# Row sums turned through DRAM and spread by a transfer, in a float32 transformer pair on one core

## The reference, cut to what matters

```python
sh1, sc1, g1, sh2, sc2, g2 = split(silu(c) @ w_mod + b_mod)      # 2048 values each
h = rms_norm(x, norm_g[0]) * (1 + sc1) + sh1
x = x + g1 * rms_norm(fourier_mix(h) @ fnet_w_out, norm_g[1])
h = rms_norm(x, norm_g[2]) * (1 + sc2) + sh2
x = x + g2 * rms_norm(square(relu(h @ w_mlp_in)) @ w_mlp_out, norm_g[3])
# second block, FoX heads: causal, so queries 0..127 see keys 0..127 only
logits = q @ k.T * scale + c[q] - c[k];  p = softmax(where(causal, logits, -inf));  o = p @ v
```

## Time and profile before

| | us |
|---|---|
| median of 3 runs | 2137.29 (2136.57 to 2138.25) |
| the profiled execution | 2136.71 |
| its span in the trace | 2135.0 |
| PE busy in it | 2092.3 |
| DVE busy | 1356.6 |
| ACT busy | 994.9 |
| TensorE clock granted, mean | 0.997 |

### The profile page before, as it was taken

One profiled execution on the slowest core, in us unless ns is written; L12 is line 12 of the kernel. 1 busy time (PEld: TensorE's weight loads), 2 busy tenths in 40 slices (PEclk: granted clock), 3 DMA queues, 4 the chain that ended last, 5 costly groups with the idle time before them and its releaser, 6 DMA issues.

```text
span 2135.0 us, 29831 instructions
## 1 busy us (share of the span) xinstructions
PE 2092.3 (98%) x11099; PEld 1762.9 (83%) x11099; DVE 1356.6 (64%) x1350; ACT 994.9 (47%) x1282; POOL 59.2 (3%) x95
## 2 busy tenths in 40 slices
PE   5999999999999999999999999999999999999999
PEld 3767878888888888887988888888888888888887
DVE  3878988887655655656767476555645655554563
ACT  4344364444543444444554567554434434343442
POOL 0010000110000000001100000000000000000000
PEclk9999999999999999999999999999999999999999
DMA  9999988887667667666665555566566656656654
GB/s 387 379 393 397 371 320 329 305 303 259 223 213 213 214 213 221 207 223 199 207 179 158 149 159 186 190 185 187 191 193 188 191 192 189 191 191 194 189 189 156
DMA packets 222842, 492.26 MB, mean 231 GB/s; under 512 B 15148, under 2 KB 15528, under 8 KB 221976
## 3 DMA queue, kind: packets, MB, share of 16 engines
q1 hardware_dynamic: 211956, 450.98, 64.9%
q0 software_dynamic: 10112, 38.79, 5.4%
q10 hardware_dynamic: 676, 1.14, 0.1%
HBM read 485.61 MB, written 5.25 MB: 230 GB/s over the span
## 4 chain that ended last, share of the span: by engine, by line
PE 87%; DVE 5%; DMA 2%; ACT 2%; issue 2%; SPq 1%; DVEq 0%; ACTq 0%
PE ps L559 43%; PE ps L521 22%; PE ps L526 11%; DVE acc L1662 3%; DMA raw<-in_w_mod_dram 2%; PE ps L543 1%; PE ps L544 1%; PE ps L545 1%; PE ps L608 1%; DMA raw<-in_w_mem_kv_dram 1%; PE ps L821 1%; PE ps L820 1%; PE ps L819 1%; PE ps L967 1%; SPq L310 1%
## 5 line engine op out<-in xcount | busy, mean ns | idle before, releaser
L1637 DVE TENSOR_TENSOR wl<-raw,wh 128x1024 fp32r<-128x1024 f32 x684 | 810.4, 1222 | 283.6 <-ACT wh L1140 281.5
L1140 ACT ACTIVATE wh<-raw 128x1024 fp32r<-128x1024 f32 x684 | 697.4, 1054 | 526.2 <-DMA raw<-in_w_down_dram 159.9
L521 PE MATMUL ps<-xt,wh 128*128 128x512 f32 x2048 | 643.7, 396 | 1.4 <-DVE xt L1897 1.4
L559 PE MATMUL ps<-wh,u 128*128 128x512 f32 x2176 | 585.1, 389 | 1.0 <-DVE u L2224 0.6
L559 PEld LDWEIGHTS ps<-wh,u 128*128 128x128 f32 x2176 | 407.3, 188 | 85.8 <-DVE u L2224 1.0
L526 PEld LDWEIGHTS ps<-xt,wl 128*128 128x128 f32 x2048 | 384.7, 188 | 90.9
L526 PE MATMUL ps<-xt,wl 128*128 128x256 f32 x2048 | 402.3, 278 | 0.0
L559 PE MATMUL ps<-wl,u 128*128 128x512 f32 x1088 | 335.2, 389 | 0.0
L521 PEld LDWEIGHTS ps<-xt,wh 128*128 128x128 f32 x2048 | 312.2, 189 | 2.8 <-issue 2.4
L559 PE MATMUL ps<-wh,xt 128*128 128x512 f32 x960 | 269.0, 394 | 3.9 <-DVE wl L1637 2.6
L559 PEld LDWEIGHTS ps<-wl,u 128*128 128x128 f32 x1088 | 204.2, 188 | 42.5
(11 more groups left out here) (303 smaller groups left out, 1493.0 us busy)
## 6 DMA issues: line engine op xcount, KB each, us to landing
raw<-in_w_mlp_in_dram SPq DMA_DIRECT2D x128, 512.0 KB, 4.0
raw<-in_w_mlp_out_dram SPq DMA_DIRECT2D x128, 512.0 KB, 4.3
raw<-in_w_up_dram SPq DMA_DIRECT2D x128, 512.0 KB, 3.8
raw<-in_w_down_dram SPq DMA_DIRECT2D x128, 512.0 KB, 3.6
raw<-in_w_mod_dram SPq DMA_DIRECT2D x126, 512.0 KB, 10.5
raw<-in_w_in_dram SPq DMA_DIRECT2D x96, 512.0 KB, 3.8
slot<-in_w_mod_dram POOLq DMA_DIRECT2D x32, 512.0 KB, 5.2
raw<-in_w_out_dram SPq DMA_DIRECT2D x32, 512.0 KB, 3.6
```

What stands on the lines that cost most here:

```text
L521: mm(ps[:, 4 * par + j, :], wh[:, at, t, j * P:(j + 1) * P], flat(xt[:, kt, :, :]), start=kt == 0, stop=kt == KT - 1, skip_group_check=True)
L559: last = mm(o, act[:, kt, z, half * P:(half + 1) * P], w, start=kt == 0 and n == 0, stop=kt == KT - 1 and n == 2, skip_group_check=True)
L1140: A(flat(wh[:, i, :, :]), tile_at(landed[0]), ACT.Copy).then_inc(sem("w_hi"), 1)
L1637: V.tensor_tensor(flat(low_at(s)), tile_at(s), flat(wh[:, i, :, :]).bitcast(F32), ALU.subtract).then_inc(sem("w_lo"), 1)
```

## The change

Sums of partial rows are made as rows: `row_sum` multiplies the accumulator by a 128 x 32 block of ones, two products of 512 columns side by side in two column quadrants. ACT copies the rows to SBUF (`summed_row`), POOL writes them to DRAM and reads them back one value per partition (`turned_row`: `shift_row` for `s2`, `bias_row` for `hb`). The gates are summed by four products side by side in one bank; DVE copies four rows (`gate_row`), POOL writes them to DRAM and reads them back into all 128 partitions (`gate_spread`), and DVE multiplies in SBUF. PE's second `mod_rows` of sh2 is gone (DVE sums those four tiles), all four first groups run without the shift (so 32 tiles are summed again, by a table), the side tiles of g2 start four groups later, sh2's first tiles are loaded ahead of the first chunks, ACT squares before it rounds the first two chunks, and the FoX heads leave out keys 128..255 for queries 0..127.

```diff
-SH2_QUADS = tuple(n for n in range(32) if n // QUAD in (0, 4))
-AGAIN = [(0, kt) for kt in range(KT)] + [(1, kt) for kt in range(KT // 2, KT)]
+SH2_QUADS = tuple(n for n in range(32) if n // QUAD == 0)
+AGAIN = [(pair, kt) for pair in range(2) for kt in range(KT)]
+AGAIN_AT = [{1: 0, 3: 1, 5: 2, 7: 3}, {1: 4, 3: 5, 5: 6, 7: 7}, {1: 8, 3: 9, 5: 10, 7: 11}, {1: 12, 3: 13, 5: 14, 7: 15},
+            {1: 16, 2: 17, 3: 18, 5: 19, 6: 20, 7: 21}, {1: 22, 2: 23, 3: 24, 5: 25, 6: 26, 7: 27}, {0: 28, 1: 29, 2: 30, 3: 31}]
-        TAIL = ([("chunk", j) for j in range(4)] + [("tile", n) for n in range(4)]
+        TAIL = ([("tile", n) for n in range(4)] + [("chunk", j) for j in range(4)]
...
+            def gate_spread(k):
+                pool.wait_ge(sem("gate_row"), k + 1)
+                pool.dma_start(gate_dram[k].rearrange("(j n) -> j n", n=GC), acc[0][0:P:QP, 0:GC]).then_inc(sem("gate_kept"), 16)
+                pool.wait_ge(sem("gate_kept"), 16 * (k + 1))
+                pool.dma_start(acc[0][:, :], gate_dram[k:k + 1, :].to_broadcast([P, D])).then_inc(sem("gate_in"), 16)
...
+            def turned_row(k, dst, src, scratch, half):
+                pool.wait_ge(sem("turn_rows"), k + 1)
+                if k:
+                    pool.wait_ge(sem("turn_in"), 16 * k)
+                pool.dma_start(scratch[half].rearrange("(j n) -> j n", n=GC),
+                               src[0:2 * QP:QP, half * MODC:half * MODC + GC]).then_inc(sem("turn_out"), 16)
+                pool.wait_ge(sem("turn_out"), 16 * (k + 1))
+                pool.dma_start(dst[:, half * CH:(half + 1) * CH], scratch[half].rearrange("(c p) -> p c", p=P),
+                               allow_slow_non_contiguous=True).then_inc(sem("turn_in"), 16)
...
-                for n, b in enumerate(banks):
-                    last = mm(ps[:, b, :], ones[:, :], acc[a][:, n * GC:(n + 1) * GC], start=True, stop=True)
+                for j in range(QUAD):
+                    last = mm(ps[j * QP:(j + 1) * QP, bank, :], ones[:, 0:QP], acc[0][:, j * GC:(j + 1) * GC], start=True, stop=True,
+                              skip_group_check=True, tile_position=(0, j * QP))
...
+            def row_sum(t, half, bank):
+                for j in range(2):
+                    last = mm(ps[j * QP:(j + 1) * QP, bank, :], ones[:, 0:QP], t[:, half * MODC + j * GC:half * MODC + (j + 1) * GC],
+                              start=True, stop=True, skip_group_check=True, tile_position=(0, j * QP))
+                last.then_inc(sem("turn_mm"), 1)
...
             def shifted_hi(r):
-                act.wait_ge(sem("a2_ready"), 2 + r // 2)
-                act.wait_ge(sem("chunk_used"), CH * G_ML1 + (12, 12, 30, 32)[r])
+                act.wait_ge(sem("turn_in"), 16 * (r // 2 + 1))
+                act.wait_ge(sem("chunk_used"), CH * G_ML1 + (28, 28, 30, 32)[r])
...
+            def summed_row(k, t, half, bank):
+                act.wait_ge(sem("turn_mm"), k + 1)
+                A(t[0:2 * QP, half * MODC:half * MODC + GC], ps[0:2 * QP, bank, :], ACT.Copy).then_inc(sem("turn_rows"), 1)
...
-                act.wait_ge(sem("hb_ready"), g // 2 + 1)
+                act.wait_ge(sem("turn_in"), 16 * (g // 2 + 3))
...
+            def gate_row(k, bank):
+                dve.wait_ge(sem("gate_mm"), k + 1)
+                V.tensor_copy(acc[0][:, 0:GC], ps[:, bank, :]).then_inc(sem("gate_row"), 1)
...
-                    if (g, i) in ((0, 6), (1, 1)):
-                        gate(0, (4, 6), 0, (g,))
+                    if (g, i) == (0, 6):
+                        gate_row(0, 4)
+                    if (g, i) in ((1, 2), (1, 5)):
+                        gate(0, 0, i // 5)
...
                         if j == 2:
-                            gate(1, (2, 6), 2 + MODN, (0,))
+                            gate_row(1, 2)
                         lo(4 + j, 4 + j, m0 + (j + 1))
+                    gate(1, 2 + MODN, 0)
                     return
...
+            def keys_of(name, tb):
+                return (tb + 1) * P if name == "fox" else S
```

More of the change, by code:

```diff
@@ L775, in first_beside @@
                     transposes(1, h, (2 + i,), drained="x1t_out")
-                if (g, i) == (1, 4):
+                if (g, i) == (1, 5):
                     pe.wait_ge(*mod_used(mod_c(C_SH2, KT - 1)))
                     pe.wait_ge(sem("evacuated"), G_ML1 + 1)
[L779 to L782, removed]
+                    row_sum(acc2, 0, 0)
                 if (g, i) == (3, 5):
@@ L785, in first_beside @@
                     pe.wait_ge(sem("evacuated"), G_ML1 + 3)
-                    mod_sum(2, 0, (1,))
-            def again_sum(pair):
[L790 to L794, removed]
+                    row_sum(acc2, 1, 0)
+            def row_sum(t, half, bank):
[3 more added lines that the diff above has]
+                last.then_inc(sem("turn_mm"), 1)
+            def again_sum(pair):
+                pe.wait_ge(sem("again_used"), KT * (pair + 1))
+                row_sum(acc[1], pair, 2 + pair)
             def mlp(G0, build, ups, between=None):
@@ L1027, in att_pv @@
                     for hd in range(4):
[L1028 removed]
+                        n = keys_of(name, tb) // P
+                        for sb_ in range(n):
                             last = mm(ps[:, 4 + tb, hd * P:(hd + 1) * P], pt[:, hd, sb_, tb * P:(tb + 1) * P], val(sb_, hd),
[L1030 removed]
+                                      start=sb_ == 0 and hd == 0, stop=sb_ == n - 1, skip_group_check=True)
                 last.then_inc(sem(name + "_pv"), 1)
@@ L1148, in hi_run @@
                 for j in range(CH):
-                    if between and j < 5:
+                    if between:
                         between(j)
@@ L1539, in soft_exp @@
                 for j in range(8):
-                    A(pr[:, j, :], pr[:, j, :], ACT.Exp, bias=nmx[:, j:j + 1],
+                    n = P if name == "fox" and j % 2 == 0 else S
+                    A(pr[:, j, 0:n], pr[:, j, 0:n], ACT.Exp, bias=nmx[:, j:j + 1],
                       accum_out=sm[:, j:j + 1]).then_inc(sem(name + "_e"), 1)
@@ L1939, in mlp_up, with mlp_down @@
                                 ALU.subtract).then_inc(sem("u_lo"), 1)
-            def mlp_down(G0, s, p, e, side, onto, first=False, last=False, tail=False, between=None):
+            def mlp_down(G0, s, p, e, side, onto, first=False, last=False, tail=False, between=None, sides=()):
                 m0 = s * 32 + p * 16 + (CH * (G0 + e) + 4)
@@ L2084, in mlp1_first @@
                         held_lo(3)
-                with dve.Fori(0, 2) as p:
-                    for e in range(2):
-                        mlp_down(G_ML1, 3, p, e, True, y)
+                for g in range(GQ):
+                    n = 2 * GQ + 2 * g
+                    mlp_down(G_ML1, 3, g // 2, g % 2, True, y, between=lambda j: side_tile(n) if j == 3 else None, sides=(n + 1,))
             def out_lo(g):
```

164 lines of the change are left out of this document (92 added, 72 removed).

## The result

The changed kernel takes 2145.44 us (median of 6 runs, 2142.77 to 2148.70) against 2137.05 for the kernel before (6 runs, 2136.55 to 2138.57): ratio 1.0035, 95% interval 1.0025 to 1.0045. That is slower by 8.4 us or 0.39% by the medians (0.35% by the ratio), where the forecast had +10.0 us; the total lies 1.3 us under the forecast of 2146.7. The total was right; two of its six terms were far off, and they cancelled.

What follows compares the result with a forecast made beforehand. PE, busy 98% of the span, was taken as the bound; +1.8 - 4.6 + 7.1 + 1.4 + 6.5 - 2.2 = +10.0 us on 2136.7 gave 2146.7, own range 2141.8 to 2152, with two in ten outside 2131 to 2155.

Steps and rivals of the forecast that it cites:

- PE work removed: First MLP loses sh2's second `mod_rows` (1.85) and 0.68 in each of four sums, -4.6 us; FoX heads -2.2 us.
- First gate and seam: Before the first MLP: DVE waits 4.8 us for the gate's trip, x1's turns start at 279.8 instead of 278.0, +1.8 us.
- The shift: Second half's 10.3 us trip stalls PE 5.3 us at chunk (4, 4), plus 1.8 half clock: +7.1 us, bounds 0 and 11.
- Tiles summed again: Groups with six tiles through two buffers: 6.9 us a cycle, 55 us against 57, PE wait of 1.4 us.
- rival (c): Load queue becomes the bound in groups with six tiles, cycle 8.3 us, 9 late: +8 us, 2155; chance 0.10.
- Second gate: Tail of the first MLP: an 11 us trip holds DVE, PE stalls 7 us, +6.5 us; bounds -2.1 and +9.
- (b): Rival: only the gates wait, the shift and the tiles summed again are covered: +1.5 us, 2138.2; chance 0.15.
- DVE's wait at the first gate: Profile sign: DVE idle 4 to 6 us before a `gate` multiply near 201, with a transfer as releaser.
- the three FoX pieces: Profile sign: the forget heads' three PE pieces take 2.6, 1.3 and 2.7 us.
- PE's hole at chunk (4, 4): Profile sign for the shift: PE idle some 5 us there, with ACT or `wl` as releaser.
- DVE's wait of 8 to 9 us in the tail: Profile sign for the second gate: DVE idle 8 to 9 us at 988.
- PE's of 7 us: Profile sign for the second gate: PE idle about 7 us before its first L918-like turn.

Runs made afterwards that it cites:

- run 11: The kernel before with only the forget heads' (FoX) part of the change: 2135.77 us, ratio 0.9990.
- run 2: The changed kernel with the first gate made as before, by full products without the trip through DRAM: 2141.18 us, ratio 1.0018.
- run 12: The kernel of run 5 with the old tail order, the first four MLP chunks ahead of sh2's tiles: 2133.93 us, ratio 0.9980.
- run 10: The changed kernel with the store of the second shift half made three times, each waited for: 2150.73 us, ratio 1.0056.
- run 3: The changed kernel with the first bias row's load issued behind again tiles 22 and 23: 2145.92 us, ratio 1.0038.
- run 8: The changed kernel with the hidden bias summed by columns as before, no bias trip, six tiles a group kept: 2148.34 us, ratio 1.0040.
- Run 9: The changed kernel with only half of each again tile loaded, 256 KB instead of 512, DVE's work unchanged: 2138.31 us, ratio 1.0002.
- run 5: The changed kernel with both gates as before and again tiles five in each up group, four in each down group: 2131.51 us, ratio 0.9970.
- run 6: The kernel of run 5 with again tiles four, four, five, five in the up groups and five, five, four in the down groups: 2137.78 us, ratio 1.0000.
- run 4: The changed kernel with again tiles five per up group, four per down group, and the bias trip behind tile 23: 2139.73 us, ratio 1.0008.

## Why the forecast was right, and where it was not

**PE work removed (-4.6 and -2.2): right.** A row sum takes 0.98 us where the columns took 1.68, and the first down group starts where it did although x1's turns were 3.25 us late, which is 1.85 + 2 x 0.70. The four sums and the gates' products took about 1.0 us each, as forecast. FoX gave 2.16 in the trace and 2.1 in run 11.

**First gate and seam (+1.8): right in mechanism, 0.8 us too small (1.4 with the 0.65 us from ahead of it).** DVE waited 4.0 us (4.8 forecast), its last sc2 tile ended at 266.9 (266.8 forecast). Behind it sh2's tiles landed later than the 6.7 us taken: `mod_rows` started at 274.7 instead of 273.5, and from `keep_busy` to the turns it was 2.9 us instead of 2.65. Without the trip the change would have gained here: run 2 puts x1's turns 1.6 us ahead of the kernel before, and run 12, where the old order takes 1.9 us back, shows that this gain comes from the tail's order.

**The shift (+7.1): the step that failed.** The forecast said that "the row is copied by 380.7" and that the trip takes 10.3 us, to 391.1. In the changed kernel (timeline of ACT):

```profile
375.98 0.59 ACT L1431 ACTIVATE acc<-ps 64x512 f32<-64x512 f32 x1 [1.29 <-PE ps L828]
381.74 1.03 ACT L1459 ACTIVATE tmp<-ps 128x1024 f32<-128x1024 f32 x1 [5.17 <-PE ps L564]
384.36 1.71 ACT L1358 ACTIVATE xt<-x1t,s 128x256 fp32r<-128x256 f32 x4 [1.59 <-DMA s<-s_turn]
```

ACT's queue was not what held the row. In the kernel before it stood 2.85 and 1.6 us for loads ahead of the roundings of 369.9 and 372.6, so the two `shifted_hi` went into idle time; the forecast took that stretch as full. Here ACT even stood 1.3 us for PE's sum. The row was copied at 376.6, 4 us sooner; the trip took 7.5 us from POOL's issue, not 10.3, as the store landed in 3.6 and the turned load in 3.6. Nothing reached PE. Run 10 shows that the queue behind the wait was right, and that the case was decided by 2.0 us.

**Tiles summed again (+1.4): mis-sized, the other failing step.** The term was a buffer's cycle of "5.6 landing, 0.1 and 1.2 of DVE: 6.9 us". DVE's adds out of one buffer start at 477.86, 483.68, 490.70, 505.22, 513.12, 520.97, 528.13 and 536.63: cycles of 5.8, 7.0, 14.5, 7.9, 7.85, 7.2 and 8.5 us. The last four add up from a landing of 6.3 at the median of these groups (5.6 was the median over the whole kernel before), 1.3 of DVE, 0.3 until POOL issues. The one of 14.5 crosses the border of the two groups, where DVE adds no tile from 495.31 to 505.22; the forecast's sum had no such cycle. POOL's hold for the bias trip is in it as well: where the hold is gone, in runs 3 and 8, it is 12.5 and 12.3. From the first tile of the second pair at 477.86 to the last one's end at 540.2 it is 62.4 us; the stretch had room for 57.

PE waited 0.24 + 2.12 + 2.24 + 1.25 = 5.85 us, and in the 5 us behind the third wait the granted clock is 0.67, up to 1.6 us more. Net of the 1.4 saved in the two bias sums the stretch costs 7.2, so 8.6 in all. Of the 1.2 us that are left, about 0.8 go at the edges of the holes. From the start of the last pair of products ahead of each hole to the next start it is 0.85, 2.74, 2.85 and 1.86 us, where a pair otherwise follows after 0.46, which is 6.46 us lost; and the pair behind each of the first two takes 0.58, another 0.24. The rest stays open.

Run 9 confirms the cost by size (7.1 us; 8.45 by its trace), runs 3 and 8 exclude the bias trip as its main cause. This is rival (c)'s size, near its cycle (it took 8.3), without rival (c)'s cause: run 5 moves more bytes a second and waits for none.

**Second gate (+6.5): right in mechanism, 2.5 us too large.** The trip took 7.2 us from the store's issue instead of 11: DVE waited 4.9 us for the broadcast and 2.9 for the second gain, which POOL could issue only behind the first multiply, as forecast. (The forecast's lower bound of such a trip adds up to 2.2 + 2.2 + 3 x 0.65 = 6.35, not 6.6, and its 2.2 is a row of SP's queue; neither moves the sum.) The half clock behind the wait was not in the sum; from the first turns to `keep_busy` PE took 3.98 us, 1.7 more than before:

```profile
1013.00:1015.00 2.00, 2.00 (x9) 1.62 (x8) 2.00 (x4) 1.51 (x3) 0.00 (x0) 0.50 0.76 288
```

**The sum.** Forecast: 1.8 - 4.6 + 7.1 + 1.4 + 6.5 - 2.2 = 10.0. Traces: 3.25 (0.65 of it from ahead of the gate) - 4.65 + 0 + 8.6 + 4.0 - 2.2 = 9.0. A cost of 7 us that did not come was replaced by one of 7 us that was not seen, so the closeness of the total is luck. In the forecast's cases it was (b) for the shift and the size of (c) for the tiles; each had been given a low chance alone, and both together none. Of the signs that the forecast named, DVE's wait at the first gate, the sums near 1.0 us and the three FoX pieces came; PE's hole at chunk (4, 4) did not; DVE's wait of 8 to 9 us in the tail was 4.9, and PE's of 7 us was 4.5.

The Trainium skill (DMA: Bandwidth & Descriptors, Anatomy of one DMA) would have a store of 8 KB from GpSimd take an estimated 2.0 us. The trace agrees for the one in the tail (1.79) and not for the one beside the loads of `fnet_w_out` (4.77): the rule was right for one of the two gates, which is why neither the forecast's 4.3 nor the Trainium skill's 2.0 fitted both. The share of the transfer engines tells the two apart here: 1.04 from 192 to 197, 0.01 from 993 to 996.

## What to carry to other kernels

A rotation of buffers is priced by the whole cycle of one buffer (landing under the load of that very stretch, its consumer's place, the way back to the issuing engine) times the tiles per buffer, against the time from the first to the last due one; 0.7 us more in each landing and one long cycle at a group's border cost 7 us here, and 1.5 us less in each landing gave them back. Replacing PE products by a trip through memory paid here only where the trip's full latency, serial behind the engine that reads it, is covered: the shift sums, wanted only after the 7.5 us, cost nothing; the gates, whose reader stood for 4 to 5 us, cost about 4 us each net of the 2.4 that they save. And an edit whose single profile looks better is not yet faster: take the timed runs.

## What the runs showed of the hardware

- The time of a small store went with the load of the transfer engines. The same 8 KB store from POOL's queue took 4.77 us beside the loads of `fnet_w_out` (share 1.04) and 1.79 us in the tail (share 0.01); 4 KB stores took 5.8 at 489.7 (share 0.97) and 1.7 at 542.3 (share 0.09). A broadcast of 1 MB landed in 8.0 and 5.1 us, a turned load of one value per element in 3.6 to 7.4.
- Holes of about the same length did not have the same effect on TensorE's clock: after 2.12 us idle at 515 the granted clock stayed at 1.00 (516 to 523), after 2.24 at 531 it was 0.50 from 532 to 535, after 2.93 at 395 in run 10 it was 0.50 for 4 us. But after 2.98 at 525 in run 2, 2.89 at 506 in run 6 and 2.98 at 536 in run 10 it stayed at 1.00 for the next 2 us and more. So the length of the hole alone does not decide it; what does stays open.
- Executions of one kernel spread unevenly: over 2.0 us in the kernel before in the first comparison but 8.5 in the last (15 runs), over 2.1 in run 5, 5.9 in the changed kernel, 7.4 in run 4 and 6.5 in run 12, whose profile, of one of its faster executions, shows hardly a wait. What makes the spread was not tested; it is why several intervals here are as wide as the term they measure.
